# Retention products from rounded parts, and the gate applied before the scale

## What is computed

```python
def head_groupnorm(o):
    of = o.astype(jnp.float32)
    mu = jnp.mean(of, axis=-1, keepdims=True)
    var = jnp.mean(jnp.square(of - mu), axis=-1, keepdims=True)
    return (of - mu) * lax.rsqrt(var + GN_EPS)
...
    scores = jnp.einsum('bhid,bhjd->bhij', qc, kc) * decay_mask[None]
    inner = jnp.einsum('bhij,bhje->bhie', scores, vc)
...
    ret = head_groupnorm(retention_chunkwise(qh, kh, vh)).reshape(B, S, RET_V_DIM).astype(x.dtype)
    y_a = (ret * jax.nn.silu(z_ret)) @ w_ret_out[l]

    a = u_val * jax.nn.sigmoid(u_gate)
    a = causal_depthwise_conv_2(a, conv_w[l], conv_b[l])      # width 31
    a = jax.nn.silu(layernorm(a, conv_ln_g[l], conv_ln_b[l]))
    y_b = (a * jax.nn.silu(z_conv)) @ w_conv_out[l]
```

## Time and profile before

| | |
|---|---|
| median of 3 runs | 838.21 us (837.5 to 838.33) |
| the profiled execution | 837.87 us, its span 836.1 us |
| TensorE busy | 827.8 us, 99% |
| VectorE busy | 731.1 us, 87% |
| ScalarE busy | 500.2 us, 60% |
| GpSimd busy | 45.4 us, 5% |

### The profile page before, as it was taken

One profiled execution on the slowest core, in us unless ns is written; L12 is line 12 of the kernel. 1 busy time (PEld: TensorE's weight loads), 2 busy tenths in 40 slices (PEclk: granted clock), 3 DMA queues, 4 the chain that ended last, 5 costly groups with the idle time before them and its releaser, 6 DMA issues.

```text
span 836.1 us, 13942 instructions
## 1 busy us (share of the span) xinstructions
PE 827.8 (99%) x5146; PEld 725.1 (87%) x5146; DVE 731.1 (87%) x1179; ACT 500.2 (60%) x804; POOL 45.4 (5%) x46
## 2 busy tenths in 40 slices
PE   8999999999999999999999999999999999999997
PEld 8999998789888888888888788998887798888886
DVE  7799899868877898888989979999999999988774
ACT  6899858576566555555565775333346675546743
POOL 0001101341100000000000000000001220000000
PEclk9999999999999999999999999999999999999999
DMA  9875675511875877777776656655454435564531
GB/s 277 256 253 169 211 245 174 146 38 45 278 232 179 261 262 263 257 256 252 238 257 218 221 185 213 202 184 169 155 198 151 152 118 200 186 231 171 188 115 50
DMA packets 129882, 164.13 MB, mean 196 GB/s; under 512 B 17407, under 2 KB 92199, under 8 KB 129703
## 3 DMA queue, kind: packets, MB, share of 16 engines
q1 hardware_dynamic: 129831, 163.45, 59.9%
HBM read 159.20 MB, written 4.23 MB: 195 GB/s over the span
## 4 chain that ended last, share of the span: by engine, by line
PE 98%; DVE 1%; DMA 1%; issue 0%; ACT 0%; DVEq 0%; SPq 0%; ACTq 0%
PE psum L695 16%; PE psum L727 14%; PE psum L728 14%; PE psum L734 14%; PE psum L704 8%; PE psum L677 6%; PE psum L686 6%; PE psum L678 6%; PE psum L1028 2%; PE psum L631 1%; PE psum L641 1%; PE psum L635 1%; PE psum L1033 1%; PE psum L915 1%; PE psum L1146 1%; PE psum L1134 1%
## 5 line engine op out<-in xcount | busy, mean ns | idle before, releaser
L1220 ACT ACTIVATE w_hi<-w_raw 128x1024 fp32r<-128x1024 f32 x255 | 266.6, 1061 | 188.2 <-PE psum L734 87.1
L1786 DVE TENSOR_TENSOR w_lo<-w_raw,w_hi 128x1024 fp32r<-128x1024 f32 x256 | 305.2, 1221 | 44.3 <-ACT w_hi L1220 42.2
L695 PE MATMUL psum<-hT,w_hi 128*128 128x512 f32 x576 | 138.9, 391 | 0.0
L695 PEld LDWEIGHTS psum<-hT,w_hi 128*128 128x128 f32 x576 | 105.4, 188 | 20.2
L727 PE MATMUL psum<-w_hi,hT 128*128 128x512 f32 x280 | 113.3, 405 | 0.0
L728 PE MATMUL psum<-w_hi,hT 128*128 128x512 f32 x280 | 109.3, 390 | 0.0
L2399 DVE SCALAR_TENSOR_TENSOR cv<-aP,par,cv 128x256 f32<-128x256 f32 x240 | 107.9, 519 | 0.0
L677 PE MATMUL psum<-hT,w_hi 128*128 128x256 f32 x432 | 107.4, 286 | 0.0
L678 PE MATMUL psum<-hT,w_hi 128*128 128x256 f32 x432 | 105.9, 283 | 0.0
L677 PEld LDWEIGHTS psum<-hT,w_hi 128*128 128x128 f32 x432 | 82.8, 192 | 0.4 <-issue 0.2
L678 PEld LDWEIGHTS psum<-hT,w_hi 128*128 128x128 f32 x432 | 82.9, 192 | 0.3 <-issue 0.2
(11 more groups left out here) (341 smaller groups left out, 1108.6 us busy)
## 6 DMA issues: line engine op xcount, KB each, us to landing
w_raw<-in_w_in_dram SPq DMA_DIRECT2D x44, 1024.0 KB, 5.1
w_raw<-in_sc_w_in_dram SPq DMA_DIRECT2D x32, 1024.0 KB, 7.9
w_raw<-in_gdn_w_in_dram SPq DMA_DIRECT2D x23, 1024.0 KB, 7.1
ada<-in_w_ada_dram SPq DMA_DIRECT2D x24, 512.0 KB, 4.8
w_raw<-in_gdn_w_out_dram SPq DMA_DIRECT2D x8, 1024.0 KB, 5.5
w_raw<-in_sc_w_out_dram SPq DMA_DIRECT2D x8, 1024.0 KB, 6.4
w_raw<-in_w_ret_out_dram SPq DMA_DIRECT2D x8, 1024.0 KB, 5.1
w_raw<-in_w_conv_out_dram SPq DMA_DIRECT2D x4, 1024.0 KB, 5.1
```

Source lines behind the costliest of these rows:

```text
L695: pe.matmul(o, w_hi[s][:, k, mine], hT[:, h * KH2 + k, :, :], start=h == 0 and k == 0, stop=False, skip_group_check=True)
L1220: act.activation((w_hi[half_slot(g, h)] if home is None else third_hi[half_slot(g, home)])[:, :, :], raw[slot][:, h * KH2:(h + 1) * KH2, : ...
L1786: return dve.tensor_tensor(o, whole, hi.bitcast(F32), ALU.subtract)
```

## The change

It does five things.

1. The values and the decayed scores get rounded and low parts too: ScalarE writes `vt_hi` from PSUM (in place of the copy to `vt`) and `st_hi`, VectorE `vt_lo` and `st_lo`. Each weighted sum is three fp32r matmuls in place of one plain float32 product.
2. VectorE takes the mean from an output and multiplies with the gate in one operation, PSUM to `vt` (`gated`); `og`, the copies to it and the eight multiplications on GpSimd are gone.
3. Root and reciprocal are taken for two heads at once, and ScalarE multiplies `vt` with the reciprocal in place (`two_heads_scaled`), heads 0 and 1 in zret's chunk 6, heads 2 and 3 in zconv's chunk 0, ahead of `split_two`.
4. The convolution's shares are 8 (v, first four chunks), 6, 6, 6, 7 (v, last four), 6 (zret); those of zconv and gates stay as written.
5. PSUM banks of v are freed by VectorE, and the semaphore `chi_ready` is now `part_hi_ready`.

```diff
-READ_BY = {name: "act" if name in ("z", "v", "zret", "zconv", "gates") else "dve" for name in ORDER}
+READ_BY = {name: "act" if name in ("z", "zret", "zconv", "gates") else "dve" for name in ORDER}
+PARTS_BY = [sum((d >= RH) + d % 2 for d in range(c + 1)) for c in range(COUNT["v"])]
...
             def weighted_sums(c):
 
                 h, t = c // NT, c % NT
-                pe.wait_ge(st_ready, min(RH, c + 1))
+                pe.wait_ge(st_ready, RH + h + 1)
                 if c >= 4:
                     pe.wait_ge(gn_ready, c - 3)
                 vh = slice(h * RDV, (h + 1) * RDV)
                 o = psum[:, 4 + c % 4, :]
-                mm = pe.matmul(o, st[:, h, t * P:(t + 1) * P], vt[:, 0, vh], start=True, stop=(t == 0))
-                if t:
-                    mm = pe.matmul(o, st[:, h, SEQ:SEQ + P], vt[:, 1, vh], start=False, stop=True)
+                for b in range(t + 1):
+                    cs = slice(t * P, (t + 1) * P) if b == 0 else slice(SEQ, SEQ + P)
+                    pe.matmul(o, st_hi[:, h, cs], vt_hi[:, b, vh], start=b == 0, stop=False, skip_group_check=True)
+                    pe.matmul(o, st_hi[:, h, cs], vt_lo[:, b, vh], start=False, stop=False, skip_group_check=True)
+                    mm = pe.matmul(o, st_lo[:, h, cs], vt_hi[:, b, vh], start=False, stop=b == t, skip_group_check=True)
                 mm.then_inc(ro_done, 1)
...
-            chunks("v", tokens_out(vt, ACT.Copy))
+            def beside_v(i, j, done):
+                c = 4 * i + j
+                if c >= RH:
+                    act.wait_ge(st_ready, RH)
+                    act.wait_ge(sco_done, RH)
+                    act.activation(st_hi[:, c - RH, :], st[:, c - RH, :], ACT.Copy).then_inc(part_hi_ready, 1)
+                if c % 2:
+                    act.wait_ge(half_done, done)
+                    act.activation(vt_hi[:, :, c // 2 * CW2:(c // 2 + 1) * CW2], psum[:, j - 1:j + 1, :], ACT.Copy).then_inc(part_hi_ready, 1)
+            chunks("v", beside_v, unroll=True)
...
+            def two_heads_std(q):
+                both = slice(2 * NT * q, 2 * NT * (q + 1))
+                act.wait_ge(gn_step, 4 * NT * (q + 1))
+                act.activation(grs[:, both], gmv[:, both, 1], ACT.Sqrt, bias=eps_n[:, :]).then_inc(gn_std, 1)
+
+            def two_heads_scaled(q):
+                act.wait_ge(gn_rec, q + 1)
+                for n in range(2 * NT * q, 2 * NT * (q + 1)):
+                    h, t = n // NT, n % NT
+                    vh = slice(h * RDV, (h + 1) * RDV)
+                    act.wait_ge(gn_ready, n + 1)
+                    act.activation(vt[:, t, vh], vt[:, t, vh], ACT.Copy, scale=grs[:, n:n + 1]).then_inc(rg_ready, 1)
 
             def beside_zret(i, j, done):
                 c = 4 * i + j
-                if c and c % 2 == 0:
-                    group_norm(c // 2 - 1)
+                if c == RH:
+                    two_heads_std(0)
+                if c == RH + 2:
+                    two_heads_scaled(0)
                 z_ret(i, j, done)
...
             def turned_pairs(i, j, done):
                 if j == 0:
-                    group_norm(RH - 1)
+                    two_heads_std(1)
                 z_conv(i, j, done)
+                if j == 0:
+                    two_heads_scaled(1)
                 split_two(j)
...
-            for n in range(NT * RH):
-                h, t = n // NT, n % NT
-                pool.wait_ge(gn_ready, n + 1)
-                vh = slice(h * RDV, (h + 1) * RDV)
-                pool.tensor_tensor(vt[:, t, vh], og[t][:, :], zr[:, t, vh], ALU.mult).then_inc(rg_ready, 1)
...
             def decayed(i, j, done):
                 c = 4 * i + j
-                conv_share(9 if c < RH else 8)
+                conv_share(8 if c < RH else 6 + c // 7)
                 if c < RH:
                     dve.wait_ge(sco_done, c + 1)
                     dve.tensor_tensor(st[:, c, :], psum[:, 4 + c, 0:3 * P], decay[:, c, :], ALU.mult).then_inc(st_ready, 1)
+                else:
+                    dve.wait_ge(part_hi_ready, PARTS_BY[c - 1] + 1)
+                    part_lo(st_lo[:, c - RH, :], st[:, c - RH, :], st_hi[:, c - RH, :]).then_inc(st_ready, 1)
+                if c % 2:
+                    dve.wait_ge(part_hi_ready, PARTS_BY[c])
+                    columns = slice(c // 2 * CW2, (c // 2 + 1) * CW2)
+                    part_lo(vt_lo[:, :, columns], psum[:, j - 1:j + 1, :], vt_hi[:, :, columns]).then_inc(bank_free, 2)
...
+            def gated(h):
+                vh = slice(h * RDV, (h + 1) * RDV)
+                dve.wait_ge(gn_step, 2 * NT * (h + 1))
+                dve.wait_ge(bank_free, 4 + FIRST["zret"] + NT * (h + 1))
+                for n in range(NT * h, NT * (h + 1)):
+                    dve.scalar_tensor_tensor(out=vt[:, n % NT, vh], in0=psum[:, 4 + n % 4, :], scalar=gmv[:, n, 0:1], in1=zr[:, n % NT, vh], op0=ALU.subtract, op1=ALU.mult).then_inc(gn_ready, 1)
 
             def group_norm(i, j, done):
                 n = 4 * i + j
                 h, t = n // NT, n % NT
+                if n == RH + 1:
+                    two_heads_inverse(0)
+                conv_share(6)
                 if n and t == 0:
-                    group_scale(h - 1)
-                conv_share(7)
+                    gated(h - 1)
                 dve.wait_ge(ro_done, n + 1)
...
             def turned_pairs(i, j, done):
+                conv_share(5 if j else 8)
                 if j == 0:
-                    group_scale(RH - 1)
-                conv_share(5 if j else 8)
+                    gated(RH - 1)
+                    two_heads_inverse(1)
                 split_two(j)
```

More of the change, by code:

```diff
@@ L161, in build @@
         freq = new("freq", [P, 1])
-        gst, gmv, grs, gnm = new("gst", [P, NT, 6]), new("gmv", [P, NT, 2]), new("grs", [P, NT]), new("gnm", [P, NT])
+        gst, gmv, grs, gnm = new("gst", [P, NT, 6]), new("gmv", [P, NT * RH, 2]), new("grs", [P, NT * RH]), None
         xn = at("xn", o_ar, [P, NT, D])
@@ L229, in build @@
         o_t = o_q + 32 * K
+        vt_hi, vt_lo = at("vt_hi", o_q + 16 * K, [P, NT, 2 * D], F32R), at("vt_lo", o_yT + 16 * K, [P, NT, 2 * D], F32R)
         st = at("st", o_t, [P, RH, 3 * P])
+        st_hi, st_lo = (at(n, o_q + 6 * s * K, [P, RH, 3 * P], F32R) for s, n in enumerate(("st_hi", "st_lo")))
         glu, rp1, rp2 = (at(n, o_t + 2 * s * K, [P, 2, SEQ]) for s, n in enumerate(("glu", "rp1", "rp2")))
@@ L233, in build @@
         cT_hi, cT_lo = at("cT_hi", o_ar, [P, KT, SEQ], F32R), at("cT_lo", o_q + 24 * K, [P, KT, SEQ], F32R)
-        og = [at(f"og{t}", o_t + (9 + 2 * t) * K, [P, RDV]) for t in range(NT)]
         zr = at("zr", o_yT, [P, NT, 2 * D])
@@ L317, in build @@
         lna_ready, lns_ready, lnz_ready = sem("lna_ready"), sem("lns_ready"), sem("lnz_ready")
-        chi_ready, cop_ready, mg_ready, mhi_ready, mop_ready = (
-            sem(n) for n in ("chi_ready", "cop_ready", "mg_ready", "mhi_ready", "mop_ready"))
+        part_hi_ready, cop_ready, mg_ready, mhi_ready, mop_ready = (
+            sem(n) for n in ("part_hi_ready", "cop_ready", "mg_ready", "mhi_ready", "mop_ready"))
         qs_done, o1_ready, gn_rec, ln_scalars = (
@@ L1648, in channels_out @@
                 return each
-            chunks("v", tokens_out(vt, ACT.Copy))
-            z_ret = tokens_out(zr, ACT.Silu)
[L1652 to L1662, removed]
+            def beside_v(i, j, done):
[8 more added lines that the diff above has]
+            chunks("v", beside_v, unroll=True)
+            z_ret = tokens_out(zr, ACT.Silu)
+            def two_heads_std(q):
[9 more added lines that the diff above has]
+                    act.activation(vt[:, t, vh], vt[:, t, vh], ACT.Copy, scale=grs[:, n:n + 1]).then_inc(rg_ready, 1)
             def beside_zret(i, j, done):
                 c = 4 * i + j
-                if c and c % 2 == 0:
-                    group_norm(c // 2 - 1)
+                if c == RH:
+                    two_heads_std(0)
+                if c == RH + 2:
+                    two_heads_scaled(0)
                 z_ret(i, j, done)
@@ L1707, in layer_norm @@
                         act.wait_ge(lnz_ready, q + 1)
-                        act.activation(cT_hi[:, pair, :], cv[:, pair, :], ACT.Copy).then_inc(chi_ready, 1)
+                        act.activation(cT_hi[:, pair, :], cv[:, pair, :], ACT.Copy).then_inc(part_hi_ready, 1)
             chunks("ret_out", layer_norm, unroll=True)
@@ L2462, in _, with two_heads_inverse @@
             chunks("v", decayed, unroll=True)
[L2464 to L2468, removed]
+            def two_heads_inverse(q):
+                both = slice(2 * NT * q, 2 * NT * (q + 1))
+                dve.wait_ge(gn_std, q + 1)
+                dve.reciprocal(grs[:, both], grs[:, both]).then_inc(gn_rec, 1)
+            def gated(h):
[4 more added lines that the diff above has]
```

(12 more changed lines are left out.)

## The result

The changed kernel takes 843.31 us, median of 6 runs (841.62 to 844.68); the kernel before takes 838.17 us on the same chip (6 runs, 837.5 to 838.56). The ratio is 1.0062, with a 95% interval of 1.0049 to 1.0075: slower by 5.1 us. The profiled execution took 844.28 us (span 842.5). The forecast was 841.8 in a range of 839.0 to 844.2, slower.

What follows compares the result with a forecast made beforehand. TensorE's matmul stream was taken to bound the kernel, VectorE close behind. 837.87 us profiled, plus 2.4 for the later mean matmul and 1.5 for the clock, gave 841.8, range 839.0 to 844.2.

Steps and rivals of the forecast that it cites:

- Products in parts: TensorE's weighted sums: 36 matmuls at 0.227 us (8.2) replace 12 plain products (10.7), making its stream 2.5 us shorter.
- 19 operations late, 6.22 us per gates chunk: VectorE in gates: 19 more convolution operations, 7.5 us late; full chunks take 6.22 us against TensorE's 5.44.
- The new wait on the scaling: In zconv's first chunk VectorE idles 3.0 us, 678.3 to 681.3, while ScalarE scales four blocks before the first turned pair.
- The second addition: GpSimd's addition in gates slows the two VectorE operations that start a pair, 1.71 us against 0.73: 1.0 more.
- The sum's time: VectorE delivers the convolution's sum at 748.65, TensorE asks at 743.8: wait 4.8 us, mean matmul 2.4 later than before.
- The lower bound: VectorE, held until its split for the third gates chunk, is still 0.9 us late: 838.8 without a clock loss.
- rival (b): VectorE is earlier than counted, ScalarE's chain at 678 being shorter or hidden: 838.3 to 839.8, middle 839.0; chance 0.15.
- rival (d): TensorE also waits for low weight halves in the last gates chunks, clock falls longer: near 844; chance 0.10.
- The clock: Behind TensorE's 4.8 us wait at the mean, 2.9 us of half-speed work lose 1.5 us, between 0 and 3.
- Rival (a): TensorE's wait for the sum comes, but the clock doesn't fall: 840.3; chance 0.22.
- (c): VectorE delivers the sum by 743.8, ten gates operations fitting beside two splits; TensorE keeps its 2.5 us: 835.4; chance 0.05.
- (e): TensorE's products in parts don't run at 0.227, but VectorE's 748.6 sets the end: time hardly moves; chance inside the forecast.

Runs made afterwards that it cites:

- e7: Changed kernel with mean matmul after ret_out's second chunk, seven convolution operations per zret chunk from the second on, scaling of heads 2 and 3 in zconv's second chunk: 835.61 us.
- e10: Changed kernel with mean matmul after ret_out's second chunk and seven convolution operations per zret chunk from the second on, scaling left where the change put it: 835.50 us.
- e3: Changed kernel with ScalarE's rounding of the first turned pairs put ahead of the scaling of heads 2 and 3 in zconv's first chunk: 843.68 us.
- e5: Changed kernel with ScalarE's scaling of heads 2 and 3 moved from zconv's first chunk to its second: 842.88 us.
- e2: Changed kernel with 20 matmuls nobody reads added on TensorE just ahead of its wait for the convolution's sum: 840.90 us.
- e6: Changed kernel with seven convolution operations in every zret chunk instead of six, eight operations back: 839.16 us.
- e8: Changed kernel with all the convolution's shares as before the change (9, then 8 in v; 7 in zret): 838.14 us.
- after: The changed kernel itself, compared with the kernel before: 843.31 us, ratio 1.0062.
- e4: Kernel before with only the change's new convolution shares in v and zret: 845.39 us.
- e9: Changed kernel with 8 matmuls nobody reads added on TensorE ahead of its wait for the convolution's sum: 842.61 us.
- e1: Changed kernel with TensorE's mean matmul, and its wait for the sum, after ret_out's second chunk instead of its first: 837.11 us.

## Why the prediction was right, step by step

- **Products in parts.** 36 matmuls stepping by 0.23 (623.35 is the first), as forecast. The gain was put at 2.5 and is 2.47. e7 and e10 show it whole: against before, their medians are 2.1 and 2.5 us shorter.
- **19 operations late, 6.22 us per gates chunk.** Measured 6.23. The anchor held: ScalarE's rounding for zconv's third chunk was forecast at 671.4, which with the start's 1.30 is 672.7, and came at 672.72; VectorE stood 0.77 there.
- **The new wait on the scaling.** 3.0 forecast, 3.11 measured, four scalings in 2.56 (forecast 2.4). Two gate products take 1.40 in one row, 0.66 from one to the next, as forecast.
- **GpSimd.** The second addition holds the pair of operations at 709.96 to 1.71, as the earlier trace rows; the first (682.30) lies beside a 1.29 us subtraction which is 1.28 elsewhere. Both as forecast.
- **The sum's time.** Forecast 748.65, with the start 749.95; measured 750.25. Of the 0.3 us between them 0.13 came with the scaling and 0.15 is the hold at 705.64. Here a step failed: the prediction took the idle in zconv for a part of the road to the sum. It isn't. VectorE is held once more, by the weights for gates' fourth chunk, and e3 and e5 show that the idle time carries nothing. By the prediction's own terms that hold ends at 746.26 - 15 x 2.72 - 2.5 + 0.2 + 1.06 + 0.04 = 704.26, and the road over the idle time reaches the same split at 703.0 + 1.14 = 704.14. The two lie 0.1 us apart, so the size came out right by luck, over the wrong road.
- **The lower bound, and rival (b).** The bound took the third gates chunk as the last place at which TensorE holds VectorE, and allowed a wait of as little as 3.4 us. The right place is the fourth, and it leaves 5.0. Rival (b), 839.0 with a chance of 0.15, had no room; e3 and e5 are (b)'s condition made true, and gave 843.7 and 842.9.
- **Low halves of weights.** The margin of 0.2 us at ret_out's first chunk, part of rival (d), held: no such wait.
- **The clock.** The fall was forecast, its price 1.5 us between 0 and 3, and it was 2.4. The return takes longer than the fall did at the kernel's end. This is the mis-sized term. The Trainium skill's page "TensorE: Matmul & The Clock Gate", Part 1, says that the return takes steady work; the rows from 750.30 to 755.1 agree, with 4.8 us. Rival (a), no fall, would be 840.3, and e2 shows what it looks like: 840.9.
- **Rivals (c) and (e).** Neither came: ten operations take 4.03 beside nothing new, and the products run at full rate.

Net: 2.4 + 1.5 = 3.9 us were forecast; 2.7 + 2.4 = 5.1 are in the traces, and the medians say 5.1.

## What to carry to other kernels

When work that is off the critical path is taken out of one stage, ask which stage gets it and whether that stage has slack: here 19 small operations left stages that could have kept at least eight of them (e6), though not all (e8), for a stage where VectorE is slower than TensorE, and the sum behind it had a margin of 2.3 us. When you look for what a delay costs, follow the queue forward to the last place where the critical engine itself holds it; everything before that drops out, idle time included. And a wait of 3 to 5 us in mid-kernel cost TensorE some 2 us more than its length here, so move the waiting matmul behind work that is ready before you shorten what it waits for.

## What the runs showed of the hardware

- **The clock's fall is not tied to a fixed time after the last matmul.** It came 3.0 us into the pause in after, 4.1 in e3, 5.0 in e4 (at its very end), only 2.1 in e5, and in e9 3.7 us after the last work, when TensorE was already at work again. Each had a pause of 5.0 (e9: 3.2). The half-speed work that followed was 4.8, 5.9, 3.4, 4.0 and 3.4 us long, so a wait cost between 1.7 and 2.9 us more. The fall in e5, whose last matmul ends at 744.42:

```profile
746.50:747.00 0.50, 0.00 (x0) 0.56 1.05 410
```

- **Short pauses may do it too.** In the profiled execution of e6 a pause of 1.9 us left the clock at 1.00 (mean of the execution 0.999), but in 8 of its 12 runs the mean clock was 0.996 or 0.997 (after's runs: 0.994 to 0.996); before shows that in 1 of 25 beside it, and e1, with a pause of 1.7 us, in none of 11. This agrees with the median, 839.16, which lies 1.4 us over the profiled 837.74. Whether the pause was longer in those runs is open; only the profiled one has a trace.
- **GpSimd holds VectorE by operand.** In e5 GpSimd's first addition fell on five convolution operations, with two inputs in SBUF, and they took 1.07 us longer than five without it:

```profile
682.11 3.13 DVE L2412 SCALAR_TENSOR_TENSOR cv<-aP,par,cv 128x256 f32<-128x256 f32 x5
...
688.63 2.06 DVE L2412 SCALAR_TENSOR_TENSOR cv<-aP,par,cv 128x256 f32<-128x256 f32 x5
```

  In after the same addition lay beside a subtraction with one input in PSUM, and cost nothing. That is what the Trainium skill's page "SBUF — State Buffer" has in its section on the two separate sides. The operation that starts a pair has only one large input, and was held all the same (1.71 against 0.73 us); the page also names a two-port mode, and no row tells whether it ran in one.
